# Differential attention scores as four 384-column matmuls on four row groups, fed by half-swapped copies of queries and upper keys

## What is computed

```python
DA_HEADS, DA_V, DA_QK = 4, 64, 32          # 4 heads, two maps a head, 32 features a map
def diff_softmax_attend(q, keys, vals, lam):
    s = jnp.einsum('bqhmd,bkhmd->bhmqk', q, keys).astype(jnp.float32) * (DA_QK ** -0.5)
    p = jax.nn.softmax(s, axis=-1)
    w = p[:, :, 0] - lam * p[:, :, 1]
    return jnp.einsum('bhqk,bkhv->bqhv', w.astype(vals.dtype), vals)
...
keys = jnp.concatenate([dk_l, dk_c], axis=1)      # 512 latent and 256 context tokens
od_l = ...                                        # 4 tiles of 128 latent queries x 768 keys
od_c = diff_softmax_attend(dq_c, dk_c, dv_c, lam) # layer 0 alone: 2 tiles x 256 keys
```

## Time and profile before

| | before |
|---|---|
| median of three runs | 3219.26 us (3217.62 to 3225.38) |
| profiled execution: span | 3213.4 us |
| TensorE busy | 2931.1 us, 91% |
| VectorE / ScalarE / GpSimd busy | 51% / 32% / 6% |
| attention stages with what fills them | about 1083 to 1253 us and 2375 to 2546 us |
| Fourier stages | about 1057 to 1083 us and 2355 to 2375 us |

### The profile page before, as it was taken

One profiled execution on the slowest core, in us unless ns is written; L12 is line 12 of the kernel. 1 busy time (PEld: TensorE's weight loads), 2 busy tenths in 40 slices (PEclk: granted clock), 3 DMA queues, 4 the chain that ended last, 5 costly groups with the idle time before them and its releaser, 6 DMA issues.

```text
span 3213.4 us, 44931 instructions
## 1 busy us (share of the span) xinstructions
PE 2931.1 (91%) x18762; PEld 2400.9 (75%) x18762; DVE 1629.9 (51%) x3421; ACT 1040.4 (32%) x2010; POOL 208.6 (6%) x270
## 2 busy tenths in 40 slices
PE   8988999999999998888799999999899797899998
PEld 6766788888977566677568888888666686578886
DVE  4333544445445255677763433333825667654444
ACT  3223433233343245343242211211415444332222
POOL 0000000000000100100000000000211246100001
PEclk9999999999999999899899999999999798899999
DMA  7434312222222110222512212121011110223221
GB/s 234 151 111 156 103 53 60 60 60 60 73 86 105 53 33 1 83 80 80 192 59 92 66 53 66 53 77 65 36 52 33 30 41 1 92 92 105 92 96 62
DMA packets 227830, 248.75 MB, mean 77 GB/s; under 512 B 5569, under 2 KB 193069, under 8 KB 226093
## 3 DMA queue, kind: packets, MB, share of 16 engines
q1 hardware_dynamic: 227628, 245.89, 23.8%
HBM read 236.43 MB, written 9.44 MB: 77 GB/s over the span
## 4 chain that ended last, share of the span: by engine, by line
PE 56%; DVE 9%; ACT 4%; issue 2%; DMA 1%; POOL 0%; ACTq 0%; SPq 0%; DVEq 0%; POOLq 0%
PE PS L2176 52%; PE PS L2180 2%; PE PS L2386 1%; ACT AR L179 1%; DVE AR L3153 1%; ACT L174 1%; DVE STAT L3089 1%; DMA WR<-in_w_in 1%; DVE AR L2898 1%; ACT EX L179 0%; DVE AR L2913 0%; DVE EX L3140 0%; DMA WR<-in_w_mod 0%; DVE AR L2909 0%; ACT STAT L179 0%
## 5 line engine op out<-in xcount | busy, mean ns | idle before, releaser
L2176 PE MATMUL PS<-HI,WC 128*128 128x512 f32 (+2 forms) x1600 | 428.0, 353 | 0.6 <-DVE WC L3134 0.6
L2176 PE MATMUL PS<-AR 128*64 128x64 f32 (+8 forms) x3756 | 315.7, 268 | 65.5 <-ACT AR L179 24.9
L2176 PE MATMUL PS<-DW,DH 128*128 128x384 f32 (+1 forms) x1344 | 355.4, 346 | 1.0 <-ACT DH L179 1.0
L2176 PEld LDWEIGHTS PS<-AR 128*64 128x64 f32 (+5 forms) x3756 | 270.7, 171 | 111.9 <-issue 33.8
L179 ACT ACTIVATE AR<-PS 128x512 f32<-128x512 f32 (+4 forms) x389 | 165.9, 453 | 552.6 <-PE PS L2176 428.2
L2176 PEld LDWEIGHTS PS<-HI,WC 128*128 128x128 f32 x1600 | 284.0, 189 | 42.5 <-DVE WC L3134 1.1
L2176 PE MATMUL PS<-LO,WC 128*128 128x512 f32 (+2 forms) x800 | 282.2, 353 | 0.0
L2176 PE MATMUL PS<-HT,WR 128*128 128x256 f32 (+1 forms) x928 | 261.4, 435 | 15.1 <-ACT EX L179 5.7
L2176 PE MATMUL PS<-WR,HT 128*128 128x128 f32 (+2 forms) x1296 | 252.0, 352 | 11.7 <-ACT AR L179 5.4
L2176 PEld LDWEIGHTS PS<-DW,DH 128*128 128x128 f32 x1344 | 240.6, 191 | 9.7 <-issue 7.1
L179 ACT ACTIVATE EX<-PS 128x256 f32<-128x256 f32 (+2 forms) x158 | 67.7, 431 | 530.6 <-PE PS L2176 530.6
(11 more groups left out here) (444 smaller groups left out, 4991.7 us busy)
## 6 DMA issues: line engine op xcount, KB each, us to landing
WR<-in_w_ffn_in SPq DMA_DIRECT2D x40, 1024.0 KB, 6.5
WR<-in_w_in_b SPq DMA_DIRECT2D x51, 512.0 KB, 6.0
WR<-in_w_mod SPq DMA_DIRECT2D x12, 2048.0 KB, 8.1
WR<-in_w_mod SPq DMA_DIRECT2D x24, 1024.0 KB, 5.3
WR<-in_w_ffn_out SPq DMA_DIRECT2D x22, 1024.0 KB, 4.9
WR<-in_w_in SPq DMA_DIRECT2D x40, 512.0 KB, 5.2
WR<-in_w_out SPq DMA_DIRECT2D x8, 2048.0 KB, 12.3
WR<-in_w_in SPq DMA_DIRECT2D x4, 2048.0 KB, 7.7
```

The costliest lines, as they stand in the source:

```text
L2176: mm = lambda o, l, r, start, stop: e.o.matmul(o, l, r, start=start, stop=stop, skip_group_check=True)
```

## The change

For each job of latent queries the 768 keys are cut into two halves of 384. Columns 0 to 383 of both maps are computed from QKT on the head's own two row groups as before. Columns 384 to 767 are computed on the other two row groups: for this QS holds the queries with partitions 0-63 and 64-127 swapped (512 columns of both f), and KS the keys 384 to 767, swapped in the same way. So a job is four matmuls of 384 columns, each with its own row group and its own PSUM bank. Jobs of the context tiles stay two matmuls of 256 columns.

QS and KS are made by four DMAs from SBUF to SBUF per layer, each from 64 partitions to the other 64: two of 2 x 512 columns and two of 2 x 384. They are written over LT (layer 0) or beside LX (layer 1), so they wait for the last of the six additions. In the plan they stand behind the additions and ahead of the loads of the DFT tables. The first job of latent queries waits for them (semaphore `swap`).

The maximum and the exponential read a map as 2 x 384 columns (one half from each bank) in place of 768 in a row; the maps are stored as 2 x 384 as well, with one of the four halves now in HNB; the transposes pick their 128 columns accordingly.

```diff
-                    a.spans, a.k0, a.nk = ([(0, 512), (512, 768)], 0, 6) if i < 4 else ([(512, 768)], 4, 2)
...
+                    f, o, s = h // 2, (h % 2) * 64, 64 - (h % 2) * 64
+                    rows = lambda t, at, m: t[at + 32 * m:at + 32 * m + 32]
+                    if i < 4:
+                        a.k0, a.nk, cols, a.need = 0, 6, slice(128 * i, 128 * i + 128), [("swap", swapped)]
+                        a.scores = [(bank(2 * m)[:, 0:384], rows(QKT, o, m)[:, f, cols], rows(QKT, o, m)[:, 2 + f, 0:384]) for m in range(2)]
+                        a.scores += [(bank(2 * m + 1)[:, 0:384], rows(QS, s, m)[:, f, cols], rows(KS, s, m)[:, f, :]) for m in range(2)]
+                        a.from_ = [PS[:, 2 * m:2 * m + 2, 0:384] for m in range(2)]
...
+            PAs = [[BR[:, 0:2, 0:384], BR[:, 2:4, 0:384]], [BR[:, 4:6, 0:384], HNB[:, 0:768].rearrange("p (b n) -> p b n", b=2)]]
+            swap_at = LT_AT if both else LX_AT[1] - 512
+            QS = AR[:, swap_at:swap_at + 1024].rearrange("p (f n) -> p f n", f=2)
+            KS = AR[:, swap_at + 1024:swap_at + 1792].rearrange("p (f n) -> p f n", f=2)
...
             th = [("rj", n)]
+            for a in (0, 64):
+                P.add("ld", "swap", QS[64 - a:128 - a, :, :], QKT[a:a + 64, 0:2, 0:512], P.count["fence"], th)
+                P.add("ld", "swap", KS[64 - a:128 - a, :, :], QKT[a:a + 64, 2:4, 384:768], P.count["fence"], th)
...
             def df_s(n, a):
                 e.wait_ge("df_e", 2 * (n - 1))
-                for lo, hi in a.spans:
-                    b = 0 if lo == a.spans[0][0] else 1
-                    for m_ in range(2):
-                        m = e.o.matmul(bank(2 * m_ + b)[:, 0:hi - lo], a.q[m_], a.k[m_][:, lo:hi], start=True, stop=True)
+                e.wait_all(a.need)
+                for o, q, k in a.scores:
+                    m = e.o.matmul(o, q, k, start=True, stop=True)
...
-                    sv = PS[:, 2 * m_:2 * m_ + 2, :].rearrange("p b n -> p (b n)")[:, 0:128 * a.nk].rearrange("p (a n) -> p a n", n=256)
-                    e.activation(a.maps[m_], sv, ACT.Exp, bias=st[:, m_:m_ + 1], scale=32.0 ** -0.5,
+                    e.activation(a.maps[m_], a.from_[m_], ACT.Exp, bias=st[:, m_:m_ + 1], scale=32.0 ** -0.5,
...
-                    sv = PS[:, 2 * m_:2 * m_ + 2, :].rearrange("p b n -> p (b n)")[:, 0:128 * a.nk]
-                    e.o.tensor_reduce(st[:, m_:m_ + 1], sv, AX, ALU.max).then_inc(sem("df_v"))
+                    e.o.tensor_reduce(st[:, m_:m_ + 1], a.from_[m_], AXY, ALU.max).then_inc(sem("df_v"))
```

More of the change, by code:

```diff
@@ L17 @@
 AX = mybir.AxisListType.X
+AXY = mybir.AxisListType.XY
 EPS = 1e-6
@@ L1556, in build, with attention_stage @@
         xneed = [("mem", 48)]
-        def attention_stage(l, tiles, QKT, DV, BR, PAs, PTds, SQ, fill):
+        def attention_stage(l, tiles, QKT, QS, KS, swapped, DV, BR, PAs, PTds, SQ, fill):
             def product(a):
@@ L1569, in attention_stage @@
                     a.i, a.h, a.l = i, h, l
-                    a.spans, a.k0, a.nk = ([(0, 512), (512, 768)], 0, 6) if i < 4 else ([(512, 768)], 4, 2)
                     n = len(jobs)
[L1572 to L1576, removed]
+                    f, o, s = h // 2, (h % 2) * 64, 64 - (h % 2) * 64
[5 more added lines that the diff above has]
+                        a.from_ = [PS[:, 2 * m:2 * m + 2, 0:384] for m in range(2)]
+                        a.maps = PAs[n % 2]
+                    else:
+                        a.k0, a.nk, a.need = 4, 2, []
+                        a.scores = [(bank(2 * m)[:, 0:256], rows(QKT, o, m)[:, f, 128 * i:128 * i + 128], rows(QKT, o, m)[:, 2 + f, 512:768]) for m in range(2)]
+                        a.from_ = [PS[:, 2 * m:2 * m + 1, 0:256] for m in range(2)]
+                        a.maps = [p[:, 0:1, 0:256] for p in PAs[n % 2]]
+                    a.t = PTds[n % 2]
                     a.v = [DV[:, a.k0 + j, 64 * h:64 * h + 64] for j in range(a.nk)]
@@ L1609, in build @@
             DV = ar.get(6 * 256).rearrange("p (i n) -> p i n", i=6)
-            PAs = [BR[:, 3 * j:3 * j + 3, 0:512] for j in range(2)]
+            PAs = [[BR[:, 0:2, 0:384], BR[:, 2:4, 0:384]], [BR[:, 4:6, 0:384], HNB[:, 0:768].rearrange("p (b n) -> p b n", b=2)]]
+            swap_at = LT_AT if both else LX_AT[1] - 512
+            QS = AR[:, swap_at:swap_at + 1024].rearrange("p (f n) -> p f n", f=2)
+            KS = AR[:, swap_at + 1024:swap_at + 1792].rearrange("p (f n) -> p f n", f=2)
             sg_at = ar.at
@@ L1885, in fill @@
                     next(filling, None)
-            attention_stage(l, [4, 5, 0, 1, 2, 3] if both else [0, 1, 2, 3], QKT, DV, BR, PAs, PTds, SQ, fill)
+            attention_stage(l, [4, 5, 0, 1, 2, 3] if both else [0, 1, 2, 3], QKT, QS, KS, 64 * (l + 1), DV, BR, PAs, PTds, SQ, fill)
             for _ in filling:
@@ L2393, in df_t @@
                 for lo in range(0, a.nk, 4):
-                    m = turn(bank(4 + lo // 4), [a.maps[0][:, j // 2, 128 * (j % 2):128 * (j % 2) + 128] for j in range(lo, min(a.nk, lo + 4))])
+                    m = turn(bank(4 + lo // 4), [a.maps[0][:, j // 3, 128 * (j % 3):128 * (j % 3) + 128] for j in range(lo, min(a.nk, lo + 4))])
                 m.then_inc(sem("df_t"))
```

## The result

The changed kernel took 3253.44 us (median of five runs, 3251.2 to 3259.25) against 3219.26 us: 34 us slower, a ratio of 1.0106 with a 95% interval of 1.0091 to 1.012. The forecast was 3252 us.

A forecast was written before the change was run, and what follows sets the result against it. TensorE, busy 91% of the span, was taken as the bound, with the table prefetch on SP's queue at stake. Loss 51 us less gain 18 us gave +33 us, 3219.3 + 33 = 3252 us; range 3236 to 3271 us.

The forecast's parts named there:

- What bounds the kernel: Whole kernel: TensorE, busy 91% of the span; SP's in-order queue prefetches the first DFT table by about 30 us.
- Part 1: Large score jobs in attention: four row groups run together, saving 0.65 us a job; gain 18 us, bounds 0 and 22.
- rival B: Score jobs: the four matmuls run in pairs, so the gain is gone and the loss stays, 3270 us; chance 0.10.
- the 4 us that were taken off: Attention: half of 13 large jobs followed by PE waits counted as lost, 6.5 x 0.65 = 4 us off the gain.
- Part 2: Attention's maximum, exponential and transposes: same instructions and elements, cut as 2 x 384; no change in time.
- Part 3: Copies ahead of the DFT tables on SP: PE stalls 22.5 us per layer, bounds 20.8 and 24.6.
- The clock: Start of each Fourier stage: half clock after the idle time, costing 3 us a layer, 0 as lower bound.
- The sum: Whole kernel: loss 51 us less gain 18 us gives +33 us, 3252 us.
- Rival C: DFT table load on SP: not held up, no stall, the gain stands alone, 3201 us; chance 0.07.
- Rival D: Copies on the queue: as slow as the spills, stall near 30 us a layer, 3267 us; chance 0.10.
- The signs: SP and PE timelines: k_dft some 2 us behind, idle 20 to 25 us, clock 0.5, attention 7 to 10 us shorter.
- the sign of being wrong: Attention stage: losing its clock more often than before, from 0.95 to 0.97, would make the forecast wrong.

The follow-up runs named there:

- scores alone: Changed kernel without the four copies, the other two matmuls reading QKT on the neighbouring head's row groups: 3197.9 us against 3217.0 us for the kernel before.
- tables first: Changed kernel with the copies behind the two k_dft loads, waiting for two of six additions, which come first: 3200.1 us against 3217.0 us for the kernel before.
- full-width kernel: Changed kernel with two unswapped copies of 128 partitions in place of four of 64, same bytes: 3246.6 us, +29.7 us against the kernel before.
- short wait: Changed kernel with the copies still ahead of the tables but waiting for two additions instead of six: 3231.9 us, +14.9 us against the kernel before.
- copies behind all tables: Changed kernel with the four copies moved behind the loads of all DFT tables, full wait kept: 3205.5 us against 3217.0 us for the kernel before.
- the two halves: Kernel before plus the four copies, read by nobody: 3270.6 us; changed kernel without copies, scores reading QKT: 3197.9 us; both against 3217.0 us.

## Why the prediction was right, point by point

- **What bounds the kernel, and that the prefetch is what is at stake:** right. The chain of waits goes through exactly the queue that was named.
- **Part 1, the scores.** 0.84 us a job was forecast, 0.86 measured, so 0.63 us saved in place of 0.65. All four groups run together; the bound of zero, and with it rival B, fell. The estimate from the Trainium skill, "TensorE: Matmul & The Clock Gate", Part 3 (0.84 us), now has its row: 0.86 us, or 2.58 / 0.86 = 3.0 times. The term of the sum was 18 us; by stages it was 6.2 + 11.0 = 17.2 in the profiled execution, and 19.1 in the medians of the scores alone. That the size came out right is in part luck: the 4 us that were taken off were for waits that only grow, but in layer 1 11.0 us arrived in the stage, all of the 16 x 0.63 us and a little more, of which up to 2 us were given back behind it. In layer 0 the loss is of another kind: right behind the first two context jobs the granted clock was low for a few us (eight records at 1113.94 took 6.19 us where the same took 3.70 at 1085.73 before). It isn't the stall that does this: with the tables first and no stall at all the same eight records took 6.13 us, while behind a stall of 22 us in the full-width kernel they took 3.70. In the three executions in which it didn't happen (short wait, copies behind all tables, full-width copies) layer 0 took 189.2 to 189.3 us, a gain of 10.0 us. But this isn't a gain that stays. The 302 us behind layer 0's attention took 304.0 to 304.5 us in these three and 300.4 to 303.1 us in the seven other kernels with the new scores; together, from the same ScalarE instruction in the Fourier stage on (1076.0 us before), it is 501.8 to 502.3 us in the three and 499.9 to 503.5 in the seven, against 509.9 before. Where the clock falls moves the time about more than it changes the sum. Why it falls at the one place or the other stays open.
- **Part 2, maximum, exponential, transposes at nothing:** right, 0.96 and 0.90 us as before.
- **Part 3, the stall.** Forecast 22.5 us a layer more than before, bounds 20.8 and 24.6; measured 24.45 - 0.78 = 23.7 and 24.24 - 0.51 = 23.7 us. The additions' 13.9 us are right (13.8 from where PE would have started). The mis-sized term is the issue: four copies took 3.1 us where 1.6 were taken from the spills (1.8 with the wake-up), because SP needed 0.61 to 0.94 us for each of these copies and not 0.4; that it isn't the 64 partitions shows in the copies of 128, 0.62 and 0.70 us. The table landed 6.5 us behind its issue, 5.1 alone, and 6.8 had been taken: the copies' bytes were not yet through. Both lay within the bound. The upper bound was added up wrongly: 5.3 + 3 + 2 is 10.3 and not 10.7 us, and 8.6 is the middle of 6.9 and 10.3. So the upper end was 24.2 us of stall and 56 us of loss; the forecast itself doesn't change.
- **The clock.** 3 us a layer were forecast; measured 3.0 and 2.5 us in the first execution, 1.4 and 2.1 in the second. It is the clock and not another wait, as the kernel with 55 additional matmuls shows.
- **The sum:** 2 x (23.7 + 2.8) = 53 us of loss against 51, 19 us of gain against 18: the two small errors cancel, and 34.2 us were measured against 33. The medians of the two halves, 53.6 and -19.1, leave 0.3 us for anything else, which is less than these medians can tell.
- **Rival C** (the other side) would have needed the table in the queue ahead of the wait. The kernel with the tables first is this case made true: 3200 us, where C gave 3201 us. **Rival D** fell: the copies landed in 3.1 to 4.5 us, not in 10.
- **The signs.** Most came: the idle time of 20 to 25 us ended by the DMA, the low clock behind it, eight records in about 0.9 us. Three were off. `k_dft` was issued 3.1 us behind the start of the copies and not 2. The attention was to be 7 to 10 us shorter in each layer; the stages were 6.2 and 11.0 us shorter. And the sign of being wrong, an attention stage that loses its clock more often, did show in layer 0 (mean granted clock 0.94, where it was 0.96) but not in layer 1 (0.99, where it was 0.98).

## What to carry to other kernels

On a queue that issues in order, a transfer that waits costs not its own time but that of everything queued behind it: before adding one, look for the next load in that queue and for how long it was prefetched. Here 0.9 MB of copies cost 26 to 27 us a layer at one place in the plan, and nothing that could be measured a few lines further down, once they waited for two additions in place of six. Behind all tables with the full wait they still cost some 7 us, because other loads stood behind them there. And when a change consists of a gain and its preparation, measure both alone; here a gain of 19 us stood under a loss of 54 us.

## What the runs showed of the hardware that I had not expected

- A copy inside SBUF from 64 partitions to the other 64 cost SP 0.61 to 0.94 us to issue, one of 128 partitions 0.62 to 0.70 us for twice the bytes; a spill of 128 partitions 0.34 and 0.43 us.
- Keeping the array busy in a stall gave the next stage its full clock (14.0 us in place of 15.4 to 17.0), but the 3.6 us less in the two stages of one pair of executions could not be found again in the total of 3250 us.
- What a stage gains by keeping its clock can be lost again behind it: layer 0's attention took from 189.2 to 193.4 us in the kernels with the new scores, and with the 302 us behind it those with 189.2 and 189.3 us were no faster than the others (501.8 to 502.3 against 499.9 to 503.5 us).
